# Seven-product blocks in PSUM for four of eight gate/up k-pairs, and w_down row by row over eight banks

## What is computed

```
h = rms_norm(x, ffn_norm)                               # (256, 2048)
x = x + (jax.nn.silu(h @ w_gate) * (h @ w_up)) @ w_down # w_gate, w_up: (2048, 5632); w_down: (5632, 2048)
return rms_norm(x, final_norm)
```

## Time and profile before

| | us |
|---|---|
| median of 3 runs | 1133.69 (1133.12 to 1133.85) |
| span of the profiled execution | 1131.9 |
| TensorE busy | 1119.1 (99%) |
| VectorE busy | 561.3 (50%) |
| ScalarE busy | 503.0 (44%) |

### The profile page before, as it was taken

How to read it: one execution, slowest core, us unless ns; L and a number is a source line. 1 busy time by engine, 2 the same in 40 slices (tenths; PEclk the granted TensorE clock), 3 DMA queues, 4 the chain that set the end, 5 groups by cost and what they waited for, 6 DMA issues and landing times.

```text
span 1131.9 us, 13061 instructions
## 1 busy us (share of the span) xinstructions
PE 1119.1 (99%) x5290; PEld 933.7 (82%) x5290; DVE 561.3 (50%) x456; ACT 503.0 (44%) x484; POOL 37.9 (3%) x44
## 2 busy tenths in 40 slices
PE   9999999999999999999999999999999999999997
PEld 6788889987888888888888888888888888888885
DVE  6444457754665544445454444444454444443453
ACT  6643446655655453343433443433434334343333
POOL 0380000000000000000000000000000000000000
PEclk9999999999999999999999999999999999999999
DMA  9766644554445556556555555555565565555552
GB/s 349 245 192 201 198 122 139 196 159 140 137 162 184 186 186 193 186 188 201 186 190 191 185 185 185 186 193 186 189 201 188 189 219 174 204 196 185 203 194 113
DMA packets 109070, 212.47 MB, mean 188 GB/s; under 512 B 4080, under 2 KB 12016, under 8 KB 108656
## 3 DMA queue, kind: packets, MB, share of 16 engines
q1 hardware_dynamic: 107040, 206.58, 55.5%
q10 hardware_dynamic: 2000, 5.46, 1.3%
HBM read 209.93 MB, written 2.10 MB: 187 GB/s over the span
## 4 chain that ended last, share of the span: by engine, by line
PE 96%; DMA 2%; ACT 1%; DVE 1%; issue 0%; SPq 0%; DVEq 0%; ACTq 0%
PE bank L1024 30%; PE bank L1026 30%; PE bank L1025 30%; PE bank L1063 2%; DMA raw<-in_w_in 2%; PE bank L1111 1%; PE bank L1203 1%; PE bank L1204 1%; PE bank L1205 1%; PE bank L1110 0%; ACT w_hi L381 0%; ACT junk L408 0%; DVE w_lo L708 0%; PE bank L1082 0%; PE bank L1128 0%
## 5 line engine op out<-in xcount | busy, mean ns | idle before, releaser
L713 DVE TENSOR_TENSOR w_lo<-raw,w_hi 128x2048 fp32r<-128x2048 f32 (+1 forms) x153 | 342.2, 2237 | 415.6 <-ACT w_hi L386 415.6
L386 ACT ACTIVATE w_hi<-raw 128x2048 fp32r<-128x2048 f32 (+1 forms) x153 | 286.2, 1871 | 427.7 <-DMA raw<-in_w_down 151.3
L1024 PE MATMUL bank<-w_hi,xT_hi 128*128 128x512 f32 (+1 forms) x1056 | 407.5, 386 | 2.8 <-DVE w_lo L708 1.8
L1026 PE MATMUL bank<-w_hi,xT_lo 128*128 128x512 f32 (+1 forms) x1056 | 405.0, 384 | 0.0
L1025 PE MATMUL bank<-w_lo,xT_hi 128*128 128x512 f32 (+1 forms) x1056 | 404.8, 383 | 0.0
L1024 PEld LDWEIGHTS bank<-w_hi,xT_hi 128*128 128x128 f32 x1056 | 198.3, 188 | 42.7 <-issue 2.4
L1026 PEld LDWEIGHTS bank<-w_hi,xT_lo 128*128 128x128 f32 x1056 | 198.2, 188 | 38.9
L1025 PEld LDWEIGHTS bank<-w_lo,xT_hi 128*128 128x128 f32 x1056 | 198.3, 188 | 38.0
L708 DVE TENSOR_TENSOR w_lo<-raw,w_hi 128x2048 fp32r<-128x2048 f32 (+2 forms) x47 | 98.7, 2101 | 97.5 <-ACT w_hi L381 97.5
L1024 PE MATMUL bank<-w_hi,hid_hi 128*128 128x512 f32 x352 | 137.0, 389 | 0.0
L1026 PE MATMUL bank<-w_hi,hid_lo 128*128 128x512 f32 x352 | 136.9, 389 | 0.0
(11 more groups left out here) (184 smaller groups left out, 585.7 us busy)
## 6 DMA issues: line engine op xcount, KB each, us to landing
raw<-in_w_gate SPq DMA_DIRECT2D x44, 1024.0 KB, 5.1
raw<-in_w_up SPq DMA_DIRECT2D x44, 1024.0 KB, 5.1
raw<-in_w_in SPq DMA_DIRECT2D x34, 1024.0 KB, 5.2
raw<-in_w_down SPq DMA_DIRECT2D x32, 1024.0 KB, 5.0
raw<-in_w_out SPq DMA_DIRECT2D x16, 1024.0 KB, 5.0
raw<-in_w_down SPq DMA_DIRECT2D x16, 768.0 KB, 4.3
raw<-in_w_in SPq DMA_DIRECT2D x8, 576.0 KB, 3.8
raw<-in_w_ukv SPq DMA_DIRECT2D x3, 1024.0 KB, 5.1
```

The costliest lines, as they stand in the source:

```text
L386: nc.scalar.activation(w_hi[n % 4][:, 0:k, :], raw[n % 4][:, 0:k, :], ACT.Copy).then_inc(hi_ready, 1)
L713: nc.vector.tensor_tensor(w_lo[n % 4][:, 0:k, :], raw[n % 4][:, 0:k, :], w_hi[n % 4][:, 0:k, :].bitcast(F32), ALU.subtract).then_inc(lo_re ...
L1024: nc.tensor.matmul(out, hi, w_h, start=start, stop=False)
L1026: return nc.tensor.matmul(out, lo, w_h, start=False, stop=stop)
```

## The change

The eight chunks of a slice are now k-pairs: chunk p holds k-tiles 2p and 2p+1 with the up and the gate columns of both, four blocks of 128x512 in a row, laid out so by the host (`w_gu`). Pairs 1, 3, 6 and 7 are plain: 24 matmuls into banks 0 to 3. Pairs 0, 2, 4 and 5 (`SUMS`) are a Strassen step over (2 k-tiles) x (up, gate) x (2 blocks of tokens): seven products in place of eight, 21 matmuls, into banks 0, 1, 2 and 4 to 7. For these, VectorE forms four sums of the weight blocks (`t_sum`: t1 and t3 together, then t2, then t4, each waiting for the one before), ScalarE and VectorE split these too (`t_hi`, `t_lo`), and three of the four bare blocks. The activations' sums are made once (`add_sums`, `split_sums`), during the output projection.

After pair 5, `mix_sums` (VectorE) combines banks 4 to 7 into `mix`, and `mix_banks` adds it into banks 0 and 1, then 2 and 3, in which pairs 6 and 7 are also accumulated. TensorE's pair 7 waits for it (`mixed`).

For w_down the hidden activations are kept once, in float32 (`hid`). Each k-tile is a chunk of 128 rows by all 2048 columns, its activations are split as it comes (`dx_hi`, `dx_lo`), and its 24 matmuls go to eight banks, three to each. The residual is added in PSUM.

```diff
@@ sizes and stage
-FB = 2 * KT // KC
+FB = KT // 2
...
-N_CHUNKS = DN0 + 4 * DB
+N_CHUNKS = DN0 + HKT
+SUMS = (0, 2, 4, 5)
+NS = len(SUMS)
@@ ScalarE
+            def keep_hidden(i, k):
...
                 for u in range(2):
...
+                    act.wait_ge(turned, i * 2 + (u - 1))
+                    nc.scalar.activation(hid[:, bass.ds(i * 4 + (2 * u - 4), 2), :].rearrange("p a b -> p (a b)"),
+                                         bank[3], ACT.Copy).then_inc(hid_kept, 1)
...
+            def prep_hi(i, q):
+
+                slot, p = (FF0 + q) % 4, q % FB
+                act.wait_ge(raw_in[slot], i * (4 * FB) + 16 * ((FF0 + q) // 4 + 1))
+                if p not in SUMS:
+                    nc.scalar.activation(w_hi[slot][:], raw[slot][:], ACT.Copy).then_inc(hi_ready, 1)
+                    return
+                s, done = SUMS.index(p), SUMS.index(p) + NS * (q // FB)
+                nc.scalar.activation(w_hi[slot][:, 1:4, :], raw[slot][:, 1:4, :], ACT.Copy).then_inc(hi_ready, 1)
+                act.wait_ge(sum_step, i * (3 * NS) + 3 * (done + 1))
+                nc.scalar.activation(t_hi[s % 2][:], t_sum[s % 2][:], ACT.Copy).then_inc(tops_hi, 1)
...
+            def ffn(i, first=False, last=False):
                 for p in range(FB):
...
+                    if p == 0 and first:
+                        for u in UNITS[FF0]:
+                            act.wait_ge(unit_filled, INDEX[u] + 1)
+                            split_pair_hi(u, bank[3])
+                    elif p == 0:
+                        keep_hidden(i, p)
+                    if p == SUMS[-1]:
+                        act.wait_ge(mix_done, i * 2 + 1)
...
+                        nc.scalar.activation(mix[:, 0, :], bank[4], ACT.Copy).then_inc(mix_first, 1)
+                    if p == FB - 1:
...
                         for b in range(TOK):
...
+                            act.wait_ge(ffn_done, i * 3 + (b + 1))
+                            nc.scalar.activation(gate[:, b, :], bank[b], ACT.Silu,
+                                                 scale=nx2.r[:, b:b + 1]).then_inc(gate_set, 1)
+                    if last and p + AHEAD >= FB:
+                        down_hi(0, p + AHEAD - FB)
+                    else:
+                        prep_hi(i, p + AHEAD)
@@ VectorE
+            def prep_lo(i, q):
+
+                n, slot, p = FF0 + q, (FF0 + q) % 4, q % FB
+                if p not in SUMS:
...
+                t1, t3, t2, t4 = (t_sum[s][:, j, :] for j in range(4))
+                b12, b22, b21 = raw[slot][:, 0, :], raw[slot][:, 2, :], raw[slot][:, 3, :]
...
+                nc.vector.tensor_tensor(t_sum[s][:, 0:2, :], raw[slot][:, 1:3, :],
+                                        b12.unsqueeze(1).to_broadcast([P, 2, COLS]), ALU.add).then_inc(sum_step, 1)
+                dve.wait_ge(sum_step, i * (3 * NS) + (3 * done + 1))
+                nc.vector.tensor_tensor(t2, t1, b22, ALU.add).then_inc(sum_step, 1)
+                dve.wait_ge(sum_step, i * (3 * NS) + (3 * done + 2))
+                nc.vector.tensor_tensor(t4, t2, b21, ALU.add).then_inc(sum_step, 1)
...
+                nc.vector.tensor_tensor(w_lo[slot][:, 1:4, :], raw[slot][:, 1:4, :], w_hi[slot][:, 1:4, :].bitcast(F32),
+                                        ALU.subtract)
+                dve.wait_ge(tops_hi, i * NS + (done + 1))
+                nc.vector.tensor_tensor(t_lo[s][:], t_sum[s][:], t_hi[s][:].bitcast(F32),
+                                        ALU.subtract).then_inc(lo_ready, 1)
...
+            def mix_sums(i):
+
+                u3_u4, v = mix[:, 1:3, :], mix[:, 3, :]
+                dve.wait_ge(mix_first, i + 1)
+                dve.wait_ge(mix_done, i * 2 + 2)
+                nc.vector.tensor_tensor(v, mix[:, 0, :], bank[5], ALU.subtract).then_inc(mix_step, 1)
...
+                nc.vector.tensor_tensor(u3_u4, ps[:, 6:8, :], v.unsqueeze(1).to_broadcast([P, 2, COLS]),
+                                        ALU.add).then_inc(mix_step, 1)
...
+                nc.vector.tensor_tensor(v, bank[7], mix[:, 1, :], ALU.add).then_inc(mix_step, 1)
+
+            def mix_banks(i):
+
+                for half, op in ((0, ALU.add), (1, ALU.subtract)):
...
+                    banks = ps[:, 2 * half:2 * half + 2, :]
+                    nc.vector.tensor_tensor(banks, banks, mix[:, 2 * half:2 * half + 2, :], op).then_inc(mixed, 1)
...
+            def ffn(i, first=False, last=False):
                 for p in range(FB):
...
+                    if p == SUMS[-1]:
+                        mix_sums(i)
+                    if p == SUMS[-1] + 1:
+                        mix_banks(i)
                     if p == FB - 1:
...
                         for b in range(TOK):
...
+                            nc.vector.scalar_tensor_tensor(out=gate[:, b, :], in0=bank[2 + b],
...
+                    if last and p + AHEAD >= FB:
+                        down_lo(0, p + AHEAD - FB)
+                    else:
+                        prep_lo(i, p + AHEAD)
@@ TensorE
+                for out, x, right in ((4, 0, "b11"), (5, 4, "t2"), (7, 3, "t1"), (6, 5, "t3"),
+                                      (0, 1, "b21"), (2, 6, "b22"), (1, 2, "t4")):
...
+                    if p == SUMS[-1] + 2 and g % 2 == 0:
+                        pe_.wait_ge(mixed, i * 2 + (g // 2 + 1))
...
+            def down_group(k, b, c, start=False, stop=False, resumed=True):
+
+                slot, toks = (DN0 + k) % 4, slice(b * P, (b + 1) * P)
+                return group(bank[4 - 4 * b + c], [dx_hi[k % 4][:, toks]], [dx_lo[k % 4][:, toks]],
+                             [w_hi[slot][:, c, :]], [w_lo[slot][:, c, :]], start, stop, resumed)
```

More of the change, by code:

```diff
@@ L670, in _ @@
-            down(0, first=True)
-            with act.Fori(1, 3) as i:
-                down(i)
-            down(3, last=True)
+            ffn(FS - 1, last=True)
+            for k in range(4):
+                if k == 0:
+                    keep_hidden(FS, k)
+                    act.wait_ge(chunk_used, DN0)
+                    act.dma_start(fnorm[:], t["final_norm"].partition_broadcast(P)).then_inc(fnorm_in, 16)
+                down_hi(0, k + AHEAD)
+            with act.Fori(1, HKT // 4 - 1) as i:
+                for k in range(4):
+                    down_hi(i, k + AHEAD)
@@ new lines, in add_residual @@
+            def add_residual(b):
+                for c in range(4):
+                    if b + c < 4:
+                        dve.wait_ge(res_done, 4 * b + c + 1)
+                    else:
+                        dve.wait_ge(chunk_used, DN0 + 4)
+                    out = bank[4 - 4 * b + c]
+                    nc.vector.tensor_tensor(out, out, xin[:, b, c * COLS:(c + 1) * COLS], ALU.add).then_inc(res_added, 1)
+            for k in range(4):
+                if k >= 2:
+                    add_residual(k - 2)
+                down_lo(0, k + AHEAD)
@@ new lines, in sums_chunk @@
+            def sums_chunk(i, p, first):
+                slot, s = (FF0 + p) % 4, SUMS.index(p)
+                start, stop = s == 0, s == NS - 1
+                bare = {"b11": 1, "b22": 2, "b21": 3}
+                tops = {"t1": 0, "t3": 1, "t2": 2, "t4": 3}
+                if first:
+                    pe_.wait_ge(xs_made, s + 1)
+                if start:
+                    if first:
+                        after(unit_act, "a", ("xs2", 5))
+                        after(unit_dve, "v", ("xt2", 3))
+                    else:
+                        pe_.wait_ge(mix_step, i * 3)
+                for out, x, right in ((4, 0, "b11"), (5, 4, "t2"), (7, 3, "t1"), (6, 5, "t3"),
+                                      (0, 1, "b21"), (2, 6, "b22"), (1, 2, "t4")):
+                    if start and out < 3:
+                        if first:
+                            pe_.wait_ge(acc_free, ACC_O + 5 + out)
+                        elif out == 2:
+                            pe_.wait_ge(hid_made, i * 2 - 1)
+                        else:
+                            pe_.wait_ge(gate_set, i * 2 - (1 if out == 0 else 0))
+                    if right in bare:
+                        j, hi, lo = bare[right], w_hi[slot], w_lo[slot]
+                    else:
+                        j, hi, lo = tops[right], t_hi[s % 2], t_lo[s % 2]
+                    mm = group(bank[out], [xp_hi[p][:, x, :]], [xp_lo[p][:, x, :]], [hi[:, j, :]], [lo[:, j, :]],
+                               start, stop and out >= 4)
+                    if stop and out in (4, 6):
+                        mm.then_inc(mix_done, 1)
+                mm.then_inc(chunk_used, 1)
@@ L1261, in _ @@
                 ffn(i)
-            def down(i, first=False, last=False):
-                for p, (k, m) in enumerate(DOWN_KT[:DB - 2] if last else DOWN_KT):
-                    if first and p == 10:
-                        pe_.wait_ge(unit_dve, DVE_UNITS + 2 * FS)
-                    chunk(DN0 + p, hid_hi, hid_lo, range(k, k + m), 0, p == 0, p == DB - 1,
```

(12 more changed lines are left out.)

457 lines of the change are left out of this document (287 added, 170 removed).

## The result

| kernel | median, us | lowest to highest | ratio to before (95% interval) |
|---|---|---|---|
| before | 1133.67 | 1133.12 to 1133.85 | |
| changed | 1189.20 | 1187.18 to 1190.95 | 1.0490 (1.0475 to 1.0505) |

The change makes the kernel 55.5 us slower. The sign was forecast, the size was not: 1170 was said, and 1189.2 lies just outside the range of 1144 to 1187. The profiled execution took 1187.18 us; its span is 53.6 us longer than that of before (1131.9).

What follows compares the result with a forecast made beforehand. TensorE bounds the kernel before; VectorE was to bound the changed slices. Slices gave +28.8 and the end -0.7, together +28, making 1161.8 us of the median; the clock's +8 made 1170, range 1144 to 1187.

Steps and rivals of the forecast that it cites:

- VectorE becomes the bound, 42.3 us against 41.7: In a slice, VectorE's summed instructions take 42.3 us, above TensorE's 41.7, so the 29.9 us saved cannot come in full.
- The walk, 46.9 us a slice: Step-by-step timing of the engines through a slice: 46.9 us against 44.4, with TensorE standing 5.2 us before chunk 7.
- the 1.8 us wait: Early in a slice, VectorE idles 1.8 us for `w_hi` of chunk 3, which ScalarE makes after two hidden copies.
- the wait ahead of chunk 7: Late in a slice, VectorE idles 0.7 us for chunk 7's `w_hi`, which follows a transfer landing at 26.6 us.
- half of the 12 stalls at 1.4 us: +8: TensorE's clock falls to 1.2 GHz in half of 12 stalls, costing 1.4 us each: +8 us.
- the opening's 1.4 us: At the kernel's opening, 24 matmuls starting at 1.2 GHz took 6.74 us instead of 5.3: 1.4 us lost.
- The rival that had all twelve fall at 1.4 to 2.7 us, 1179 to 1194: The clock falls in every TensorE stall, 12 falls of 1.4 to 2.7 us: 1179 to 1194 us, chance 0.24.
- First and last slice, +8.0 and -1.7: The first slice takes 52.4 us, 8.0 more than before; the last, with cheap chunks behind it, 42.7, 1.7 less.
- its stall in chunk 1: In the first slice, TensorE stands 5.2 us in chunk 1 until VectorE has split pair 6.
- w_down "covered", 0: In w_down, VectorE's and ScalarE's work, residual additions included, fits into each chunk's 5.44 us: no time added.
- a window of w_down with TensorE waiting: A sign in the profile after the change that would show the prediction wrong; TensorE was to have no idle time there.
- The end, -0.7: At the kernel's very end, the addition of 0.69 us leaves the path: -0.7 us.

Runs made afterwards that it cites:

- experiment 4: Against the changed kernel, ScalarE makes the second hidden copy after the high part of chunk 3 instead of before it; 1189.03 us.
- experiment 2: Against the changed kernel, TensorE runs 20 matmuls that nothing reads in its stall ahead of chunk 7; 1172.49 us, ratio 1.035.
- experiment 3: Against the changed kernel, w_down's two groups of residual additions come one preparation earlier in VectorE's order; 1182.10 us, ratio 1.043.
- experiment 5: Changed kernel with mixing straight behind its sums, hidden copies split and residual additions earlier: 1160.99 us; also with ten matmuls filling the stall ahead of chunk 0: 1159.63 us.
- the same move: `mix_banks` straight behind `mix_sums`, ahead of the next slice's chunk 0: 1170.07 us against the changed kernel; with three pairs and two other order changes 1128.71 us.

## Why the prediction was right in its sign and short in its size

- **VectorE becomes the bound, 42.3 us against 41.7.** The prices were right, each instruction on its line, but this sum doesn't explain the slowdown: 42.3 is still under the 44.4 of a slice before, so by itself it would have made the slices faster. What costs the time is the loop of experiment 4, through TensorE, a transfer, ScalarE and VectorE's order.
- **The walk, 46.9 us a slice.** Right to 0.1 us once the clock is held (46.92, experiment 2), stall included (4.82 to 5.02 for 5.2). The reason given for the 1.8 us wait, as a price on the path, was wrong (experiment 4): only the wait ahead of chunk 7, at the ring, counts.
- **The clock: "half of the 12 stalls at 1.4 us: +8".** This is the step that failed most. The walk itself gives eleven long stalls, ten ahead of chunk 7 and one in the first slice; these and the one of w_down make the trace's twelve, and the clock fell in all. Ten cost 20.5 us (experiment 2), w_down's 2.0 (6.1 less the stall of 4.1), and the first slice's other one about 1.6 (0.31 of a window of 5 us whose PEclk was 0.69): 24 in all, so this term was 16 too low. Two things were wrong in it. The share was a coin toss where the row of before had a fall after 3.0 us and the stalls were 5.2. And the opening's 1.4 us was the wrong price: behind a stall, 24 matmuls took 7.4 us (588.58 to 596.01) for 5.44, 2.0 lost. The rival that had all twelve fall at 1.4 to 2.7 us, 1179 to 1194, with a chance of 0.24, was the case that came.
- **First and last slice, +8.0 and -1.7.** 55.1 for 52.4 and 42.7 for 42.7. The first slice's two stalls, 4.2 and 5.0 us, each had a fall of the clock behind it, 3.8 us by the prices above. Without them it is 51.3, so the walk of the first slice was 1.1 us too long: its stall in chunk 1 was 4.2 us and not 5.2.
- **w_down "covered", 0.** Wrong, +6.1 measured, and the prediction had named a window of w_down with TensorE waiting as a sign against it. I compared the work for each k-tile with its time and didn't walk the first four: the additions stand in VectorE's list behind a preparation that waits for a transfer (experiment 3, 7.1 us back).
- **The end, -0.7.** -0.8.

The sum, with the measured terms in the places of mine, is for the span 1159.9 + 24 + 4.1 for the stall in w_down = 1188. The span was 1185.5; of the 2.5 us between them 1.4 are the gain ahead of the slices, which I didn't have, and 1.1 the first slice's walk.

Two things stay open: how the clock ran in the two quick executions of experiment 5, which had no trace, and how near a slice with four pairs comes to TensorE's 41.7 us if transfers had a fifth slot or less work stood between `w_hi` and `mix_banks`; no kernel changed the ring.

## What to carry to other kernels

Before saving work on the engine that bounds, sum what the saving adds on each other engine for one turn of the loop; here three seven-product pairs fit (38.0 us under 42.4) and a fourth (42.3 over 41.7) cost far more than it had saved. The sum is not enough, since 42.3 is still under the old 44.4: also follow the loop through every engine and transfer, and look at what stands ahead of the item that TensorE waits for. Price a new stall of TensorE of some microseconds with the clock behind it, here 2.0 us on each of 5. Walk the first turns after a change of stage, since a steady rate that fits says nothing about an item that is queued behind a late transfer. A change of order is worth what the present balance makes it: the same move gave 19 us with four pairs and took 1.1 us a slice with three.
